# A six-slot panel ring with low parts in place, and a reordered opening, in a two-layer mixer followed by a state-space block

## The reference, cut to what matters

```python
c_act = jax.nn.silu(c)
for l in range(2):
    mod = c_act @ w_mod[l] + b_mod[l]                    # 1024 x 6144: shift1, scale1, gate1, shift2, scale2, gate2
    h = rms_norm(x, norm1) * (1.0 + scale1) + shift1
    proj = h @ w_in                                       # keys, values, queries, pool input, gates
    mix = concatenate([pool_mixer(u), sparse_attention(q, k, v, gates)]) @ w_out
    x = x + gate1 * mix
    h2 = rms_norm(x, norm2) * (1.0 + scale2) + shift2
    x = x + gate2 * (square(relu(h2 @ w_ff1)) @ w_ff2)    # 1024 -> 4096 -> 1024
# second block: u = h @ w_in_2; state-space branch, dilated attention, gated mix @ w_out_2,
# layer norm, the same kind of feed-forward, layer norm
```

## Time and profile before

| | |
|---|---|
| Median of three runs | 1370.56 us (1369.36 to 1371.61) |
| The profiled execution | 1369.93 us, of it 1368.1 us from the first to the last instruction |
| Mean granted TensorE clock | 0.944 |
| TensorE busy | 1270.2 us (93%) |
| VectorE busy | 937.6 us (69%) |
| ScalarE busy | 620.8 us (45%) |
| Moved from memory | 245.58 MB, 180 GB/s over the span |

### The profile page before, as it was taken

The page is one execution under the profiler, slowest core; times in us unless marked ns, Lnnn a source line. Parts: engine busy times, 40 slices in busy tenths (PEclk is TensorE's granted clock), DMA queues, the critical chain, the costliest instruction groups (busy, mean ns, idle before and its releaser), DMA issues.

```text
span 1368.1 us, 21735 instructions
## 1 busy us (share of the span) xinstructions
PE 1270.2 (93%) x8834; PEld 1162.2 (85%) x8834; DVE 937.6 (69%) x1223; ACT 620.8 (45%) x828; POOL 38.4 (3%) x42
## 2 busy tenths in 40 slices
PE   6699999999998989899999998998889998999997
PEld 6587897999988779799998997886769987899996
DVE  5778868887875687775557559987865653755553
ACT  2444225444444522454444444468875532644432
POOL 1001200000000130000000000000000000000000
PEclk8699699999999989999999999999889999999999
DMA  9534554776744064465555642356744451555530
GB/s 381 214 132 154 185 199 165 281 285 242 283 155 154 31 243 156 166 216 184 184 184 215 208 154 99 120 197 205 231 159 143 155 177 60 185 196 185 186 140 31
DMA packets 43621, 247.69 MB, mean 181 GB/s; under 512 B 4160, under 2 KB 12368, under 8 KB 15520
## 3 DMA queue, kind: packets, MB, share of 16 engines
q1 hardware_dynamic: 43104, 244.57, 49.7%
q0 software_dynamic: 448, 2.14, 0.5%
HBM read 245.58 MB, written 1.11 MB: 180 GB/s over the span
## 4 chain that ended last, share of the span: by engine, by line
PE 69%; DVE 17%; DMA 6%; ACT 5%; issue 2%; SPq 0%; POOL 0%; DVEq 0%; ACTq 0%
PE bank L388 14%; PE bank L390 13%; PE bank L389 13%; PE bank L687 12%; PE bank L688 6%; DVE w_lo L383 4%; DMA arena<-in_modw 2%; DVE arena L1017 2%; ACT w_hi L378 2%; PE bank L809 2%; DVE arena L1916 1%; DVE macc L1017 1%; DMA arena<-dscr 1%; DMA raw<-in_panels 1%; PE bank L477 1%
## 5 line engine op out<-in xcount | busy, mean ns | idle before, releaser
L383 DVE TENSOR_TENSOR w_lo<-raw,w_hi 128x2048 fp32r<-128x2048 f32 x170 | 388.7, 2290 | 186.3 <-ACT w_hi L378 185.9
L378 ACT ACTIVATE w_hi<-raw 128x2048 fp32r<-128x2048 f32 x170 | 324.1, 1910 | 229.7 <-PE bank L390 117.3
L687 PE MATMUL bank<-act,w_hi 128*128 128x512 f32 x768 | 280.2, 406 | 12.3 <-DVE act L1038 5.5
L388 PE MATMUL bank<-act,w_hi 128*128 128x256 f32 x800 | 238.1, 298 | 8.6 <-DVE act L1038 7.2
L388 PE MATMUL bank<-ff_hi,w_hi 128*128 128x256 f32 (+1 forms) x816 | 230.3, 282 | 1.8 <-issue 1.0
L389 PE MATMUL bank<-act,w_hi 128*128 128x256 f32 x800 | 230.7, 288 | 0.0
L390 PE MATMUL bank<-ff_hi,w_lo 128*128 128x256 f32 (+1 forms) x816 | 230.7, 283 | 0.0
L389 PE MATMUL bank<-ff_lo,w_hi 128*128 128x256 f32 (+1 forms) x816 | 230.6, 283 | 0.0
L390 PE MATMUL bank<-act,w_lo 128*128 128x256 f32 x800 | 230.5, 288 | 0.0
L688 PE MATMUL bank<-act,w_lo 128*128 128x256 f32 x768 | 217.7, 283 | 0.0
L687 PEld LDWEIGHTS bank<-act,w_hi 128*128 128x128 f32 x768 | 146.1, 190 | 51.4 <-issue 10.9
(11 more groups left out here) (320 smaller groups left out, 1767.0 us busy)
## 6 DMA issues: line engine op xcount, KB each, us to landing
raw<-in_panels SPq DMA_DIRECT2D x170, 1024.0 KB, 4.9
arena<-in_modw SPq DMA_DIRECT2D x48, 1024.0 KB, 6.8
mixf<-dscr SPq DMA_DIRECT2D x8, 512.0 KB, 6.0
arena<-dscr SPq DMA_DIRECT2D x8, 512.0 KB, 4.9
mixf<-dscr SPq DMA_DIRECT2D x8, 256.0 KB, 6.3
arena<-dscr SPq DMA_DIRECT2D x8, 256.0 KB, 6.4
cst<-in_cst SPq DMA_DIRECT2D x1, 1251.5 KB, 7.6
arena<-in_x SPq DMA_DIRECT2D x1, 1024.0 KB, 5.0
```

The lines of the kernel that those rows point to most:

```text
L378: nc.scalar.activation(w_hi[slot(k)][:, :], raw[:, k % RAW, :], ACT.Copy).then_inc(hi_done, 1)
L383: nc.vector.tensor_tensor(w_lo[slot(k)][:, :], raw[:, k % RAW, :], w_hi[slot(k)][:, :].bitcast(F32), ALU.subtract).then_inc(lo_done, 1)
L388: nc.tensor.matmul(o, wh, xh, start=start, stop=False, skip_group_check=skip)
L687: nc.tensor.matmul(bank[4 + c][:, :], wh[:, s:s + P], act2[:, kc, :, :], start=kc == 0, stop=False)
```

## The change

- The two raw slots and four low slots become one ring of six slots; the low part is written over the raw panel in its own slot. A panel keeps its slot until TensorE has used it. Panel k may be fetched when TensorE has used panel k-6 (first six: at once). There are still ten buffers of a panel.
- SyncE's order of panels and modulation units is written anew. Hardware loops run over three feed-forward passes at a time (two iterations in place of six).
- In the opening the constants are fetched in two parts, the second at the end; the seven units that VectorE now uses stand in one run, two of them (4 and 5) in ring slots 4 and 5; unit 2 is used by TensorE and unit 3 by VectorE. ScalarE copies `x` out of PSUM and makes its small masks afterwards. The high part of panel 1 is made after the root of the first norm, its low part after the norm.
- `lc` (436 KB, GpSimd's queue) waits for the fifth unit of the opening as well.

```diff
-RAW = 2
+RING_W = 6
...
-        raw = sb("raw", [P, RAW, PANEL])
+        with nc.sbuf_tensor("raw", [P, RING_W, PANEL], F32) as raw:
+            pass
+        ring_w = sb("ring_w", [P, RING_W, PANEL], F32R)
         w_hi = [sb(f"w_hi{i}", [P, PANEL], F32R) for i in range(SPLIT)]
-        w_lo = [sb(f"w_lo{i}", [P, PANEL], F32R) for i in range(SPLIT)]
...
+        def place(m, k):
+
+            return divmod(4 * (m.c if isinstance(m, Turn) else m) + k, RING_W)
...
         def load(sp, m, k):
 
-            sp.wait_ge(lo_done, 4 * m + k - RAW + 1)
-            sp.dma_start(raw[:, k % RAW, :], a["panels"][4 * m + k]).then_inc(raw_ready[k % RAW], 16)
+            n, at_slot = place(m, k)
+            if n:
+                sp.wait_ge(split_free, SPLIT + 4 * m + k - RING_W + 1)
+            sp.dma_start(w_raw(m, k), a["panels"][4 * m + k]).then_inc(raw_ready[at_slot], 16)
...
         def sp_layer(sp, l, ahead):
 
             m = 11 * l
-            load(sp, m, 2)
-            load(sp, m, 3)
             if l == 0:
                 load_mod(sp, l, 8)
-            if l == 0:
                 load_mod(sp, l, 9)
-            for k in (4, 5, 6):
-                load(sp, m, k)
+            load(sp, m, 6)
+            load(sp, m, 7)
             if l == 0:
                 load_mod(sp, l, 10)
-            load(sp, m, 7)
             load(sp, m, 8)
+            load(sp, m, 9)
             if l == 0:
                 load_mod(sp, l, 11)
-            for k in (9, 10, 11):
-                load(sp, m, k)
+            load(sp, m, 10)
             load_mod(sp, l, 12)
+            load(sp, m, 11)
             load_mod(sp, l, 13)
+            load(sp, m, 12)
             load_mod(sp, l, 14)
-            load(sp, m, 12)
             load_mod(sp, l, 15)
             load(sp, m, 13)
-            for u in (16, 17, 18):
-                load_mod(sp, l, u)
+            load_mod(sp, l, 16)
             load(sp, m, 14)
+            load_mod(sp, l, 17)
+            load(sp, m, 15)
+            load_mod(sp, l, 18)
+            load(sp, m, 16)
             load_mod(sp, l, 19)
-            load(sp, m, 15)
+            load(sp, m, 17)
             load_mod(sp, l, 20)
             load_mod(sp, l, 21)
-            for k in (16, 17, 18):
+            for k in (18, 19, 20, 21):
                 load(sp, m, k)
-            with sp.Fori(1, FF_STEPS // 2 - 1) as i:
-                load(sp, m + i, 15)
-                if ahead:
-
+            with sp.Fori(0, FF_PASSES) as i:
+                for n in range(1, 4):
+                    mm = Turn(i, m + n)
+                    load(sp, mm, 18)
                     for mp in range(2):
-                        sp.wait_ge(mod_used, MOD_PANELS * l + 20 + 2 * i + mp + 1)
-                        sp.dma_start(modw[:, mp, :], a["modw"][MOD_PANELS * l + 20 + 2 * i + mp]).then_inc(modraw[mp], 16)
-                for k in (16, 17, 18):
-                    load(sp, m + i, k)
+                        if ahead:
+
+                            u = MOD_PANELS * l + 20 + 2 * n + mp + 6 * i
+                            sp.wait_ge(mod_used, u + 1)
+                            sp.dma_start(modw[:, mp, :], a["modw"][u]).then_inc(modraw[mp], 16)
+                        load(sp, mm, 19 + mp)
+                    load(sp, mm, 21)
...
-            nc.vector.tensor_tensor(w_lo[slot(k)][:, :], raw[:, k % RAW, :], w_hi[slot(k)][:, :].bitcast(F32),
+            nc.vector.tensor_tensor(w_lo(m, k), w_raw(m, k), w_hi[slot(k)][:, :].bitcast(F32),
                                     ALU.subtract).then_inc(lo_done, 1)
...
             rsqrt(link, rs[:, :], bank[6][:, 0:T], 1.0 / D, cst[:, C_EPS:C_EPS + 1]).then_inc(rs_done, 1)
+            if q == 0:
+                split_hi(act, 0, 1)
...
             dve_norm(dve, 2 * l, 0, 0)
-            for k in (2, 3):
+            for k in (2, 3) if l else (1, 2, 3):
                 split_lo(dve, m, k)
...
-            sp.dma_start(cst[:, :], a["cst"]).then_inc(cst_loaded, 16)
...
+            sp.dma_start(cst[:, 0:C_COS], a["cst"][:, 0:C_COS]).then_inc(cst_loaded, 16)
+
+            sp.dma_start(modw_x[:, 1, :], a["modw"][3]).then_inc(first_raw[1], 16)
+            sp.dma_start(modw[:, 0, :], a["modw"][0]).then_inc(modraw[0], 16)
+            sp.dma_start(modw_x[:, 0, :], a["modw"][2]).then_inc(first_raw[0], 16)
+            sp.dma_start(modw[:, 1, :], a["modw"][1]).then_inc(modraw[1], 16)
+            for u in range(2):
+                sp.dma_start(raw[:, 4 + u, :], a["modw"][4 + u]).then_inc(first_raw[2 + u], 16)
+            for u in range(2):
+
+                sp.wait_ge(first_done, 2 + u)
+                sp.dma_start(modw[:, u, :], a["modw"][6 + u]).then_inc(modraw[u], 16)
+                if u == 0:
+                    load(sp, 0, 0)
+            for k in range(1, 4):
+                load(sp, 0, k)
+            for u in range(2):
+                sp.wait_ge(first_done, 4 + u)
+                load(sp, 0, 4 + u)
+            sp.dma_start(cst[:, C_COS:CN], a["cst"][:, C_COS:CN]).then_inc(cst_loaded, 16)
...
+            act.wait_ge(c_loaded, 16)
+            nc.scalar.activation(cact[:, :], ccol[:, 0:KC], ACT.Silu).then_inc(cact_ready, 1)
+            for kc in range(KC):
+
+                act.wait_ge(x_turned, kc // 2 * 2 + 2)
+                nc.scalar.activation(x[:, kc, :], bank[kc // 2][:, (kc % 2) * T:(kc % 2 + 1) * T], ACT.Copy).then_inc(x_ready, 1)
+            act_squares(act, 0)
...
+            first_unit(0, (first_raw[1], 16), modw_x[:, 1, :], macc[:, :, :], 1, True)
+            first_unit(1, (modraw[0], 16), modw[:, 0, :], first_sums[:, 0:2, :], 0, True)
+            first_unit(2, (modraw[1], 16), modw[:, 1, :], first_sums[:, 0:2, :], 1, False)
+            first_unit(3, (first_raw[2], 16), raw[:, 4, :], first_sums[:, 2:4, :], 0, True)
+            first_unit(4, (first_raw[3], 16), raw[:, 5, :], first_sums[:, 2:4, :], 1, False)
+            first_unit(5, (modraw[0], 32), modw[:, 0, :], first_sums[:, 4:6, :], 0, True)
+            first_unit(6, (modraw[1], 32), modw[:, 1, :], first_sums[:, 4:6, :], 1, False)
+            dve.wait_ge(first_done, 7)
+            dve.sem_inc(mod_used, 8)
+            dve.sem_inc(mod_links, 24)
+            split_lo(dve, 0, 0)
```

More of the change, by code:

```diff
@@ L176, in build @@
         act_ready = sem("act_ready")
-        raw_ready = [sem(f"raw_ready{i}") for i in range(RAW)]
+        raw_ready = [sem(f"raw_ready{i}") for i in range(RING_W)]
         hi_done = sem("hi_done")
@@ L705, in pe_ff @@
                 pe_mod(pe, 12 * l + 10, macc, MOD_AT + 40)
-            with pe.Fori(1, FF_STEPS // 2 - 1) as i:
-                up(m + i, k0 + 1, j0 + 2 * i + 1, 1)
-                down(m + i, k0 + 2, j0 + 2 * i, 0, False, False)
-                up(m + i, k0 + 3, j0 + 2 * i + 2, 0)
-                down(m + i, k0 + 4, j0 + 2 * i + 1, 1, False, False)
-                if mods == "ahead":
-                    pe_mod(pe, 12 * l + 10 + i, macc, MOD_AT + 40 + 4 * i)
+            with pe.Fori(0, FF_PASSES) as i:
+                for n in range(1, 4):
+                    mm, j = Turn(i, m + n), j0 + 2 * n + 6 * i
+                    up(mm, k0 + 1, j + 1, 1)
+                    down(mm, k0 + 2, j, 0, False, False)
+                    up(mm, k0 + 3, j + 2, 0)
+                    down(mm, k0 + 4, j + 1, 1, False, False)
+                    if mods == "ahead":
+                        pe_mod(pe, 12 * l + 10 + n + 3 * i, macc, MOD_AT + 40 + 4 * n + 12 * i)
             e = m + FF_STEPS // 2 - 1
@@ L991, in ff_schedule @@
             step(m, j0 + 1, k0 + 1, 1, None, (k0 + 5, k0 + 6), 1)
[L992 to L994 removed]
+            with eng.Fori(0, FF_PASSES) as i:
+                for n in range(1, 4):
+                    mm, j = Turn(i, m + n), j0 + 2 * n + 6 * i
+                    step(mm, j, k0 - 1, 0, k0 - 2, (k0 + 3, k0 + 4), 3 * i + n)
+                    step(mm, j + 1, k0 + 1, 1, k0, (k0 + 5, k0 + 6), 3 * i + n)
             e = m + FF_STEPS // 2 - 1
@@ L1003, in dve_mod @@
         def dve_mod(dve, pair, o, half):
-            dve.wait_ge(modraw[half], 16 * pair if not isinstance(pair, int) or pair else 16)
+            dve.wait_ge(modraw[half], 16 * pair - 16)
             unit = modw[:, half, :].rearrange("p (b k n) -> p b k n", b=2, k=4)
@@ L1413, in finish @@
         def finish(sp):
-            for k in range(2, 6):
+            for k in range(6, 22):
                 load(sp, M2, k)
-            with sp.Fori(0, 4) as i:
-                for k in (6, 7, 8, 9):
-                    load(sp, M2 + i, k)
             load(sp, M2, 22)
@@ L1438, in finish @@
                         fetch(sp, e)
-            with sp.Fori(7, 19) as i:
-                for k in (6, 7, 8, 9):
-                    load(sp, M2 + i, k)
+            for k in range(34, 82):
+                load(sp, M2, k)
             for half in range(2):
@@ L2182, in _, with first_unit @@
             link = Chain(dve, dve_links, DVE_LINKS)
-            for kc in range(KC):
```

(26 more changed lines are left out.)

100 lines of the change are left out of this document (57 added, 43 removed).

## The result

| | Before | After |
|---|---|---|
| Median | 1369.96 us (1365.85 to 1371.61, 4 runs) | 1390.93 us (1385.71 to 1395.23, 4 runs) |
| The profiled execution | 1369.93, span 1368.1 | 1389.74, span 1387.7 |
| Mean granted TensorE clock | 0.944 | 0.946 |
| PE, DVE, ACT busy | 1270.2, 937.6, 620.8 us | 1272.1, 935.2, 621.4 us |

After takes 1.0156 times as long as before (1.0113 to 1.0199): slower by 21 us, where +16 was forecast. The change is under 2%, but its interval lies wholly above 1. No engine has noticeably more work.

What follows compares the result with a forecast made beforehand. TensorE's waits for late panels early in both layers could be won; VectorE's waits for modulation units at the output rows, without slack, lost. -10.5 - 6.6 - 0.9 + 30 + 4.2 = +16 on 1369.9: 1386 us, range 1371 to 1394.

Steps and rivals of the forecast that it cites:

- The opening: Start of layer 0: units land earlier, TensorE starts at 37.1, panel 2 at 54.9 instead of 65.4; -10.5 us.
- The front of layer 1: Panel 4 is fetched long ahead, so TensorE's wait of 4.7 and the lower clock behind it go; -6.6 us.
- The -0.9 on `ff_lo`: Second block: a wait that hangs on a late panel goes; -0.9 us (0 to -1.5).
- The output rows: Both layers: units 17 and 19 stand behind panels waiting for slots, so TensorE waits; +14.9 us each, +30 in all.
- The estimate by the Trainium skill: DMA at fixed 2.0 us plus bytes by 436 GB/s: 1.1 less lost per layer, next term nearly vanishes; 1380.
- the row: Profile row on transfers: 4.8 us alone, 6.9 for a unit fetched just behind a panel; the prediction's chosen basis.
- The feed-forward of layer 0: Six passes: the first unit stands behind a waiting panel, mod starts 6.4 late, TensorE waits 0.7 each; +4.2 us.
- the row of 8.6: Layer 0's feed-forward: profile row of another such unit taking 8.6 us; at that price the term would be +11 or so.
- Layer 1's loop: Layer 1's feed-forward loop: no units there, so no loss was counted.
- At nothing: Low part in place, loops of three passes, second part of `cst`, later masks on ScalarE: all costed at zero.
- the gains win: Rival: `mod(9)` and `mod(11)` at the output rows never wait, no losses, 1352 us; chance 0.08.
- the feed-forward loses more: Rival: layer 0's feed-forward costs 11 in place of 4.2, 1393 us; chance 0.22 shared with little from the opening.

Runs made afterwards that it cites:

- e9: e3 with panel 1's high part ahead of the root and its low part ahead of the first norm, as before the change; 1353.52 us, 0.989 of before.
- r1: The changed kernel once more, unaltered; one execution, 1391.5 us.
- e5: e3 with panel 4 of layer 1 fetched only once that layer's low part of panel 2 is made, as before the change; 1357.46 us, 0.991 of before.
- e3: The changed kernel with the edits of e1 and e2, and layer 1's units 22 and 23 fetched ahead of the feed-forward loop; 1352.33 us, 0.9871 of before.
- e1: The changed kernel with units 17 and 18 fetched ahead of panel 14 and unit 19 ahead of panel 15, both layers; 1363.61 us, 0.9956 of before.
- e4: The changed kernel with unit 19 alone fetched ahead of panel 16; 1376.51 us, 1.0055 of before.
- e2: The changed kernel with both units of each layer 0 feed-forward pass fetched ahead of that pass's four panels; 1381.84 us, 1.0096 of before.
- r2: e3 once more, unaltered; one execution, 1354.46 us.
- e8: e3 with x copied out of PSUM by VectorE again, ahead of its first unit, not by ScalarE; 1351.38 us, 0.9865 of before.
- e6: e3 with the constants fetched whole behind x, not in two parts; 1358.43 us, 0.9913 of before.

## Why the prediction was right, and where its terms were off

The forecast of 1386 (1371 to 1394) stood against 1390.93, and its mechanism is what the runs show: the gains are there, and SyncE's order loses more. By its own steps:

**The opening, -10.5.** -10.9 at panel 2. The steps shown above came within half a microsecond, from the first transposes (7.01, forecast 6.7) to the last unit (29.3 against 29.6). Two reasons had not been argued: how panel 1's low part fills a hole of VectorE (e9), and a further -1.8 behind panel 2. Of that 1.5 is clock: before, the wait of 4.2 has 3.4 us at 0.5 behind it, and the profiled execution of after, with a wait of 2.8, has none. It is no sure gain, since r1, the same kernel, does show 3.4 us at 0.5 from 54.8 on, and has -0.3 in place of the -1.8.

**The front of layer 1, -6.6.** -7.4. The place and the size held, and e5 gives the cause: it takes back 5.2 of the 6.6 that e3 gains there. The rest goes with the clock, 6.8 us at 0.5 behind the wait of before and 3.4 behind that of e5. The -0.9 on `ff_lo` in the second block can't be told from the -0.4 of that whole stretch.

**The output rows, +14.9 in each layer.** +13.5 and +13.4 (e1: 27.3 for both). TensorE's waits were forecast as 2.8 over the old 0.35, and 8.5; they are 3.16 and 8.51 in layer 0. The longer waits are 2.8 + 8.0 = 10.8 of the 13.5, so 2.7 is left for the clock, where 14.9 less 10.8 had 4.1: the mis-sized part. Of the 2.7, 1.5 lies between the two waits (the stretch between them takes 18.36 us and not 8.84, 9.5 more for a wait of 8.0 more), with 3.4 us at 0.5 from 179.3 on; 1.2 lies behind the second, with 6.8 us at 0.5 from 192.9 on. The prediction had 1.6 and 2.5 for these two, so it is the second that was too large. A wait was missed, that of `mod(10)`: hidden here, and in e4, where it is not, TensorE waits 4.93 and 1.81. The estimate by the Trainium skill, "DMA: Bandwidth & Descriptors", section "Anatomy of one DMA", would have taken 1.1 off each layer and most of the next term: 1380. That section gives its figures for transfers that GpSimd issues, and these are issued by SyncE. The median panel lands after 4.8 us and the median unit after 6.9 in the profile of after, and TensorE's long wait came out as the row has it, 8.51 for 8.5, so the row was the better base.

**The feed-forward of layer 0, +4.2.** This is the term that was most mis-sized: 9.2 in the loop of the profiled execution, 9.1 by e2, and 7.3 in r1. Two things. Five of the six waits are 0.68 to 0.86, by and large the 0.7 forecast, but the start of the matmul behind one is set back by more: it comes 957 to 1137 ns after the start of the one ahead, in place of 120, and with what follows each such pass costs 0.9 to 1.1. And one pass of six is another case: its unit keeps VectorE for 7.59 us in place of 6 and TensorE waits 2.40, with 3.4 us at 0.5 from 281.7 on; this pass costs 4.2. In r1 it waits 2.11 with no lower clock behind and costs 2.4, in e4 2.05 and 2.3, and in e1 two passes wait 1.05 and 1.81, so it is no accident of one execution. The prediction knew the row of 8.6 for such a unit but priced all passes by the median. Its figure for that row, "+11 or so", does not follow from its own steps either: 8.6 and the 0.4 between the two issues, less 0.9 and 5.7, are 2.4 a pass, 14 for six. The slow pass did wait 2.4, but it was one and not six.

A further 1.0 of the table's 10.4 lies ahead of the loop, behind the second norm: in after 6.8 us at 0.5 from 210.0 on, where before has 3.4. It is not a cost of the order, since r1 has 3.4 there too, and e5 and r2, which have neither wait at the output rows, have 6.8.

**Layer 1's loop, "no units there".** True of the loop and wrong for its end. Units 22 and 23 stand behind the last loads of the loop. They go out 24.5 us later than before (744.27 against 719.74), when the whole is 17.4 us late, and `pe_mod` waits for them. The sum did not hold this. The stretch of TensorE's work around it takes 14.67 us in after and 14.76 in e4, 13.06 to 13.16 in r1, e1 and e2, and 12.03 in before and in e3. So the wait costs 1.0 to 1.1, and in after and e4 3.4 us at 0.5 behind it cost 1.6 more. The row of after:

```profile
744.27 0.81 SPq L350 DMA_DIRECT2D arena<-in_modw  x2
...
762.09 1.11 PE L509 MATMUL bank<-cst,macc 128*128 128x1 f32 x8 [1.47 <-DVE macc L1055]
```

**At nothing.** The low part in place (2288 ns against 2290), the copies of `x` (e8) and the loops of three passes (the 168.13 us of e2 and e3) cost nothing that shows. No engine waits for the second part of `cst` in after.

The terms in one line: forecast -10.5 - 6.6 - 0.9 + 30 + 4.2 = +16; by the trace -12.7 - 7.4 - 0.4 + 27.0 + 10.4 + 2.8 = +19.7, with 0.1 of rounding in it. What the forecast missed is 6.2 around the loop and 2.8 at the end of layer 1's, less 3.0 at the output rows and 2.5 on the gains. So the mechanism and its main term held, but that the sum came within 4 us of the trace is in part luck: misses of 9.0 one way and 5.5 the other. The rival "the gains win" was refused for the right reason and became true once the order was mended (e3). The rival "the feed-forward loses more", 1393 with 11, came near the size of that term by luck: it had six slow passes where the runs have one slow pass, a higher cost of the others and some lower clock.

## What to carry to other kernels

- When loads of two kinds share one queue that is issued in program order, every load that waits for a buffer holds back all that stand behind it. Give a deeper buffer and a new issue order separate trials: here the ring and the opening were worth 1.3%, and the order that came with them cost 39 us. Moving the small, urgent loads ahead of the ones that wait for slots gave it all back.
- Price such an order load by load: when is the buffer of the one ahead free, plus a transfer, against when the reader asks. Do it for each load in the chain, since the second latest takes over once the latest is mended (e4), and also for what stands behind a loop.
- Where a wait recurs in a loop at the edge of its slack, a median transfer is the wrong price: here one pass of six cost 2.3 to 4.2 us in three executions, and the others about 1.0 each, against 0.7 for each in the forecast.

## What the runs showed of the hardware that was not expected

The same wait is followed by different clocks. Before panel 2 TensorE waits 2.7 to 3.0 us in ten profiled executions with the same order at this place. The granted clock behind it was 1.0 throughout in after, e1, e2 and e4, 0.5 (1.2 GHz) for 3.4 us in e3, e5, e8, r1 and r2, and 0.5 for 6.8 us in e6. The stretch from there to the same instruction some 33 us later takes 32.36 us in after, 33.87 in e3 and 35.07 in e6. So some 1.5 to 2.7 us of a difference between two executions can be this alone, and a clock term behind a wait of 3 us belongs in the range rather than in the sum. Within the ten the waits of 2.67 to 2.85 us are the four without lower clock, and those of 2.97 to 2.99 the six with it. But e9, with another order ahead of its wait of 2.44, has 3.4 us at 0.5 behind it. And behind the wait of L719 after layer 0's second norm, 2.75 to 2.77 us in all thirteen profiled executions, 0.5 lasts 3.4 us in nine and 6.8 in four (after, e2, r2, e5), and the length of the wait does not tell them apart.

The largest such differences lie elsewhere. The stretch ahead of layer 1's output rows (489.22 to 540.12 in before, 50.90 us) in after and in r1, one kernel, in the columns of the earlier trace rows:

```profile
492.50:543.90 51.40, 44.55 (x287) 39.69 (x286) 40.50 (x64) 11.74 (x19) 12.14 (x8) 0.87 0.30 108
490.84:546.08 55.24, 50.50 (x286) 44.53 (x285) 40.71 (x64) 11.74 (x19) 12.14 (x8) 0.75 0.27 101
```

The same work takes 3.9 us more at a mean clock of 0.75 than at 0.87. In e3 and r2, one kernel too, it takes 51.24 and 53.99. Layer 0's counterpart (130.02 to 187.44 in before, 57.42 us) takes 57.23 in e3, 58.08 in r2 and 54.58 in e5, which has the same code up to there. Why the clock falls differently there is not shown. A difference of 4 us between two profiled executions of this program therefore proves nothing by itself; it has to be placed in the stretch that the edit touches.

A lone transfer of a megabyte, 4.8 us as a rule, now and then takes longer: panel 26 in the loop of after took 6.4 (266.28 to 272.69) and the unit behind it 7.9. In the same pass of r1 the panel took 4.9 and the unit was late all the same. Instruction fetches (two queues of the profile) fall into that pass and not into the last three of the loop, in after and in r1. They also fall into the first and the third pass, which have waits of 0.68 to 0.74, so they alone do not mark the slow one; the cause was not tried.
